# A two-layer hybrid decoder step: layer 0's SSM tables on VectorE, modulation blocks issued earlier, the softmax and gelu stage in another order

## The reference

```python
mod = silu(c) @ w_ada + b_ada;  shift, scale, gate = split(mod, 3)
h = rms_norm(x, norm_g) * (1 + scale) + shift
q, k, v, za, u, zs = split(h @ w_in)              # 512,128,128,512,512,512 columns
ya = windowed attention with sinks(rope(q), rope(k), v)     # prompt, and samples with a cache
# SSM: 32 groups of 16 channels, 64 complex states
abar = exp(a * dt);  bb = coef * b                # coef from a and abar
h_t = abar * h_{t-1} + bb u_t;  y = Re(c h_t) + d * u
y = gelu(y);  y = y * sigmoid(y @ w_glu + b_glu)
x = x + gate * (concat(ya * silu(za), y * silu(zs)) @ w_out)
```

## Time and profile before

| | |
|---|---|
| median of three runs | 457.63 us |
| the profiled execution | 457.97 us |
| its span on the core | 456.2 us |
| TensorE busy (matmuls) | 379.3 us, 83% |
| VectorE busy | 320.4 us, 70% |
| ScalarE busy | 199.9 us, 44% |
| GpSimd busy | 143.1 us, 31% |
| mean granted clock of TensorE | 0.934 of 2.4 GHz |

### The profile page before, as it was taken

How to read it: one execution, slowest core, us unless ns; L and a number is a source line. 1 busy time by engine, 2 the same in 40 slices (tenths; PEclk the granted TensorE clock), 3 DMA queues, 4 the chain that set the end, 5 groups by cost and what they waited for, 6 DMA issues and landing times. The chain is left out here.

```text
span 456.2 us, 8245 instructions
## 1 busy us (share of the span) xinstructions
PE 379.3 (83%) x3114; PEld 320.7 (70%) x3114; DVE 320.4 (70%) x670; ACT 199.9 (44%) x429; POOL 143.1 (31%) x153
## 2 busy tenths in 40 slices
PE   3997289999755993946979967799997999899894
PEld 2444279889652983634869866699996879688893
DVE  1547989488999547298667885536578966986763
ACT  3635084353431226137514345634651348583442
POOL 4400000999930049994069950000000000000320
PEclk9999769999988997987998987999998998999999
DMA  8798878967139537932197407139099628923303
GB/s 270 224 329 294 185 269 238 139 123 229 49 70 279 97 59 220 375 76 63 35 295 255 93 0 214 53 97 175 4 225 205 155 41 235 309 61 86 94 0 116
DMA packets 124869, 72.27 MB, mean 158 GB/s; under 512 B 63129, under 2 KB 111349, under 8 KB 124734
## 3 DMA queue, kind: packets, MB, share of 16 engines
q1 hardware_dynamic: 112462, 65.74, 55.0%
q10 hardware_dynamic: 12368, 6.00, 5.5%
HBM read 64.74 MB, written 6.59 MB: 156 GB/s over the span
## 5 line engine op out<-in xcount | busy, mean ns | idle before, releaser
L655 PE MATMUL bank<-h_hi,w_hi 128*128 128x320 f32 x448 | 146.8, 328 | 22.0 <-DVE w_lo L1598 13.6
L655 PE MATMUL bank<-h_lo,w_hi 128*128 128x320 f32 x448 | 142.0, 317 | 0.0
L655 PE MATMUL bank<-h_hi,w_lo 128*128 128x320 f32 x448 | 141.8, 317 | 0.0
L655 PEld LDWEIGHTS bank<-h_hi,w_hi 128*128 128x128 f32 x448 | 87.6, 196 | 32.0 <-DVE w_lo L1598 16.3
L1598 DVE TENSOR_TENSOR w_lo<-raw,w_hi 128x1024 fp32r<-128x1024 f32 x50 | 67.7, 1354 | 30.3 <-ACT w_hi L1196 30.2
L655 PEld LDWEIGHTS bank<-h_lo,w_hi 128*128 128x128 f32 x448 | 87.7, 196 | 0.2
L655 PEld LDWEIGHTS bank<-h_hi,w_lo 128*128 128x128 f32 x448 | 87.4, 195 | 0.0
L1196 ACT ACTIVATE w_hi<-raw 128x1024 fp32r<-128x1024 f32 x50 | 52.6, 1052 | 37.3 <-PE bank L655 31.3
L2125 POOL TENSOR_TENSOR ga<-xT,fing 128x320 f32<-128x320 f32 x4 | 3.8, 950 | 160.5 <-DVE xT L2002 160.5
L2106 POOL TENSOR_TENSOR pt<-Apow,Csb 128x288 f32<-128x288 f32 x64 | 52.6, 842 | 2.5
L655 PE MATMUL bank<-R,cT 128*32 128x512 f32 x128 | 24.1, 722 | 13.0 <-DMA R<-in_w_ada 12.9
(11 more groups left out here) (266 smaller groups left out, 665.7 us busy)
## 6 DMA issues: line engine op xcount, KB each, us to landing
R<-in_w_ada SPq DMA_DIRECT2D x32, 512.0 KB, 6.6
raw<-in_w_in SPq DMA_DIRECT2D x32, 256.0 KB, 6.0
raw<-in_w_ada SPq DMA_DIRECT2D x14, 512.0 KB, 5.5
raw<-in_w_in SPq DMA_DIRECT2D x14, 512.0 KB, 5.7
raw<-in_w_out SPq DMA_DIRECT2D x32, 128.0 KB, 3.1
raw<-in_w_out SPq DMA_DIRECT2D x16, 256.0 KB, 4.1
R<-in_w_in SPq DMA_DIRECT2D x4, 512.0 KB, 6.9
raw<-in_w_glu SPq DMA_DIRECT2D x4, 512.0 KB, 8.3
```

What stands on the lines that cost most here:

```text
L655: return nc.tensor.matmul(out_, lhsT, rhs, start=start, stop=stop, skip_group_check=free)
```

## The change

- **Tables of layer 0.** Gm of layer 0 is computed on VectorE by `carriers(q)`, four calls of five 128x576 operations each, in place of GpSimd. Three calls follow rope 0, 1 and 2, the fourth follows the modulation of layer 1. WB and Gm use three products in place of four for a complex product, with sums prepared beforehand (`Asd`, `Cdif`, `outputs_summed`). Bblk of layer 0 is copied by ScalarE. GpSimd prepares only layer 1, behind `H_ready` and, for WB, behind the last `mix_ready` of layer 0.
- **Start.** `ssm_sines` and `powers` come ahead of the wait for the spread root; `inputs_scaled` and all `turned_inputs` come after the last `h_lo`. The second half of u0 and u1 comes ahead of turning C and the sinks.
- **Modulation and transfers.** The block (0, 4) is loaded behind zs0 in place of zs1, in layer 1 (1, 4) behind za0 in place of za2; `load_quad` comes ahead of `y_turns`; layer 0's skewing all comes behind zs1. K0 of layer 0 is formed ahead of za1.
- **Softmax and gelu.** ScalarE stores the state ahead of the second exponentials. VectorE does the first gelu steps ahead of the first normalization and of silu 5. PT4, PT5 and the turned modulation 5 come behind glu; layer 1's modulation 2 comes one unit earlier.

```diff
-QUAD_LOADS = ({"q1": 0, "za2": 1, "zs1": 2, "zs3": 3, "glu1": 4, "out5": 5}, {"za2": 0, "glu1": 1})
+QUAD_LOADS = ({"q1": 0, "za2": 1, "zs0": 2, "zs3": 3, "glu1": 4, "out5": 5}, {"za0": 0, "glu1": 1})
-SKEW_AT = (["zs0", "zs0", "zs0", "zs0", "zs1", "zs1", "zs1", "zs1"],
+SKEW_AT = (["zs1"] * T,
...
+            def carriers(q):
+                i0, shape = 4 * q, [P, 4, T + 1, GC]
...
+                step.add(tt(im, A(Asd[:, 1]), C(Csb[:, 0, 0]), ALU.mult))
+                step.add(tt(t, A(Apow[:, 0, 1]), C(Csb[:, 0, 1]), ALU.mult))
+                own(tt(t2, A(Apow[:, 0, 0]), C(Cdif), ALU.mult))
+                own(tt(re, im, t, ALU.add))
+                if q < 3:
+                    own(tt(im, im, t2, ALU.add))
...
                 newton(l + 1)
+                if l == 0:
+                    powers()
                 dve.wait_ge(*work.ready(l, "rb"))
...
                 if l == 0:
+                    inputs_scaled()
+                    for m in range(4):
+                        lo_part(0, m + 2)
+                        turned_inputs(m)
...
                     rope(m)
+                    if l == 0:
+                        carriers(m)
                 lo_part(l, 9)
                 if l + 1 < DEPTH:
                     modulation_of(l + 1, 0)
+                if l == 0:
+                    carriers(3)
...
                 modulation_of(l, 4)
-                normalize(0)
-                silu(5, "zs1", gs[:, 1, :])
-                lo_part(l, 17)
-                normalize(1)
                 dve.wait_ge(y_back, (l + 1) * 64)
...
                 gelu_argument(0)
                 gelu_argument(1)
-                silu(6, "zs2", gs[:, 2, :])
-                lo_part(l, 18)
+                normalize(0)
+                silu(5, "zs1", gs[:, 1, :])
+                lo_part(l, 17)
                 gelu_product(0)
                 gelu_product(1)
                 gelu_argument(2)
                 gelu_argument(3)
+                normalize(1)
+                silu(6, "zs2", gs[:, 2, :])
+                lo_part(l, 18)
+                if l + 1 < DEPTH:
+                    modulation_of(l + 1, 2)
                 gelu_product(2)
                 gelu_product(3)
+                silu(7, "zs3", gs[:, 3, :])
+                for m in range(MT):
+                    gelu_lo(m)
```

More of the change, by code:

```diff
@@ L638, in _ @@
                     u_turns(l)
+                if unit in QUAD_LOADS[l]:
+                    load_quad(l, QUAD_LOADS[l][unit])
                 if unit == "zs3":
@@ L1400, in _ @@
                         .then_inc(y_out, 16)
[L1401 to L1406, removed]
                 act.wait_ge(*work.ready(l, "at4"))
@@ L1418, in _ @@
                         .then_inc(state_stored, 16)
-                gelu_square(0)
-                gelu_square(1)
-                gate(6, "zs2")
-                hi_part(l, 18)
-                gelu_tanh(0)
-                gelu_tanh(1)
+                exponentials(1)
+                gate(4, "zs0")
+                hi_part(l, 16)
                 if l + 1 < DEPTH:
@@ L1723, in _ @@
                         else:
-                            powers()
-                            inputs_scaled()
-                            for n in range(2):
-                                turned_inputs(n)
                             modulation_of(0, 2)
@@ L1752, in _ @@
                         .then_inc(ada.emptied(0, "sinks"), 1)
-                    for m in range(4):
-                        lo_part(0, m + 2)
-                        turned_inputs(m + 4)
+                    outputs_summed()
                     dve.wait_ge(rest_in, 16)
@@ L2086, in all_turned @@
-                def all_turned():
-                    for n in range(8):
-                        turned(n)
-                if before is not None:
-                    pool.wait_ge(*work.ready(before, "y3"))
+                X, Y = flat(Csb[:, own_, 0]), flat(Csb[:, own_, 1])
+                Ar, Ai = flat(Apow[:, own_, 0]), flat(Apow[:, own_, 1])
+                Bsum, Bdif = flat(Bsb[:, own_, 0]), flat(Bsb[:, own_, 1])
+                pool.wait_ge(ssm_ready, 1)
+                pool.wait_ge(wb_ready, l * 8)
@@ L2114, in prepare @@
-                if before is not None:
-                    pool.wait_ge(*work.ready(before, "pvs"))
-                    all_turned()
-            prepare(0, None)
-            for before in range(DEPTH - 1):
-                step.restart()
-                prepare(before + 1, before)
+                    t, t2 = (pt[:, q, 0:2 * (T + 1) * GC].rearrange("p (i s c) -> p i s c", i=2, s=T + 1)
+                             for q in range(2))
+                    re, im = (Gm[:, r, i0:i0 + 2] for r in range(2))
@@ L2123, in _ @@
+            for l in range(1, DEPTH):
+                prepare(l)
             for k in range(KT):
```

245 lines of the change are left out of this document (139 added, 106 removed).

## The result

The changed kernel takes 441.84 us (median of 4 runs, 440.94 to 444.44) beside 457.71 us of the kernel before (4 runs, 456.24 to 462.36): ratio 0.9646, 95% interval 0.9566 to 0.9725. It is faster, by 15.9 us. The same kernel was timed again later (six runs): 444.24 us, ratio 0.9766 (0.9718 to 0.9815). So its gain is 11 to 16 us, and single edits are compared best within one set of runs. The repeat was expected at 440 to 443 us and came out above that. Medians here are over all runs; the ratios leave out runs that are over 1.5% above the fastest of their kernel. The profiled execution took 441.92 us, span 440.0.

The account below looks back on a forecast made before the run. No engine bounds the whole: TensorE is busy most of the span and stops at a few places of layer 0. Terms -3.7 + 9.4 - 16.5 + 0.3 - 11.2 + 2.5 = -19.2, from 457.97 us to 439 us, range 430 to 451.

Parts of the forecast that it names:

- step 3: k to `carried`: scan shorter without GpSimd's tables beside it, block (0, 4) in time; -16.5 us, bounds -18 and -8.
- steps 4 and 5: `carried` to y3: late skewing, +0.3 us; y3 to values: earlier work and blocks, -11.2 us, bounds -18 and -3.
- Start: Start to u2: u0 4.3 us later, last modulation earlier, u2 at 63.9 not 67.61; -3.7 us, bounds -6 and 0.
- u2 to k: `carriers` on VectorE, 3.75 us a call, delays k from 105.7 to 111.4; +9.4 us, bounds 0 to +21.
- Out stage: Values' end to layer 0's sum of squares: no term of its own, left at the 40.1 us of before.
- Layer 1: Layer 1: state stored ahead of exponentials, zs3 waits 3.2 us more; +2.5 us, bounds -1 and +6.
- dear tables: Rival: `carriers` cost 6 us a call, all through S4 and the scan, +9; 448 us, chance 0.22.
- That the blocks land late: Rival: blocks load only after the one before is used, so 4.49 and 7.01 us waits stay; 451 us, chance 0.06.
- y was back in time: Answers the rival that VectorE stands at `y_back`, with work queued behind, and the change loses; 463 us, chance 0.05.
- more gain: Rival: zs3 doesn't wait (-4), no clock loss at 42 (-1.8), layer 1 free (-2.5); 431 us, chance 0.15.

Follow-up runs that it names:

- experiment 5: Changed kernel with sines and `powers` back behind the normalisation, tables still on VectorE: 442.74 us, beside 444.24 for the changed kernel in the same set.
- experiments 3 and 4: Changed kernel with, first, layer 0's Gm on GpSimd in five-operation form without `carriers`: 438.11 us; second, three `carriers` calls one place earlier: 438.18 us.
- experiment 1: Changed kernel plus 40 GpSimd multiplies that nothing reads, between layer 0's reading tables and the scan's end: 465.38 us, ratio 1.0145.
- experiment 2: Changed kernel with modulation blocks loaded at their old places, skewing split over zs0 and zs1, y's way back ahead of block (1, 2): 455.16 us.
- experiment 7: Changed kernel with block (1, 2)'s load issued behind y's transfers on SyncE, not ahead: 442.69 us, ratio 0.9669.
- first execution: First profiled execution of the changed kernel, without further edit: 441.92 us.
- second execution: Another profiled execution of the same changed kernel, from its later repeat, whose median was 444.24 us.
- experiment 8: Changed kernel with GpSimd starting layer 1's WB when pvs is there, as before, not behind the mix: 443.92 us, ratio 0.9700.
- experiment 6: Changed kernel with the old softmax and gelu order in both layers: 442.04 us; with the new order in layer 0 only: 439.12 us.

## Why the prediction was right

Forecast 439.0 us with 430 to 451; measured 441.84, and 444.24 later. The kernel is faster, as the chance of 0.92 had it, and both medians lie in the range, the second just past the forecast's own range of 434 to 444. The mechanism of the large term (step 3) was right; two smaller terms were too hopeful (steps 4 and 5), and a stage that was put at no change gave 3 us back, which was luck.

1. *Start.* -3.7 forecast, -3.4 measured; u0 started at 40.8 and not 42.2. Right in sum, wrong in what brings it. I had `powers` ahead of `normed` as half of the gain. With `powers` late and the scaled inputs and tables still moved, u2 starts earlier still (61.56 to 63.12), so it was those that had held up the last modulation; `powers` early costs 1 to 3 us (experiment 5).
2. *u2 to k.* +9.4 forecast; 111.0 less 64.2 is 46.8, before 38.0: +8.8. The price of a call was as forecast. Of the three stops, two came with the releasers named: 2.01 us for `HY` (h0; forecast 2.7) and 2.73 us for the modulation (forecast 4.4); the third, for rope2 (1.2), is 0.3 us at most. It is the price of the change, and experiments 3 and 4 take 3 to 9 us of it away.
3. *k to `carried`.* -16.5 forecast, measured 31.2 us after 48.5: -17.3. Block (0, 4) was issued at 124.6 and no wait stood behind za2 or zs0. By experiment 1 GpSimd's idleness gives the scan; by experiment 2 that alone would leave TensorE waiting 7.51 us for the block. The Trainium skill (SBUF — State Buffer, SBUF: two separate sides) has a VectorE instruction with two SBUF inputs and a GpSimd instruction that reads SBUF block each other; the trace agrees, with 213 against 601 ns for the same instruction (experiment 1).
4. *`carried` to y3.* The step that failed. Forecast +0.3, measured +3.5. It had one term, skewing that lands a microsecond late; no wait for Toep stands there in the trace. Block (1, 2)'s load was weighed only as a risk for y's way back, and put at nothing for TensorE. 2.5 us are the stop, 0.9 a wait for the modulation at 145.06. Without the load the stop goes, but the time stays (experiment 7).
5. *y3 to the values.* Forecast -11.2 us, measured -6.0 in the first execution and -6.8 in the second. In size this is the largest miss, 5.2 and 4.4 us. The wait ahead of zs3 was forecast at 6.3 and is 6.19. Not foreseen: a wait of 1.92 us for turned probabilities, and smaller ones; TensorE idles 9.2 us of the stage, and 10.0 in the second execution, with 1.5 us for gelu's `h_lo` (up to 3.5 us in other profiles). And the clock: with 0.83 over the stage the same work took 51.5 us in the first execution, beside 49.3 before; in the second it took 49.9.
6. *Out stage*, which the forecast left at 40.1: 36.6 and 37.4. These unforeseen 3 us cover more than half of what step 5 lacks. Experiment 8 shows one part of it, the rest is open.
7. *Layer 1.* +2.5 forecast, +1.6 and +2.4 measured; up to +5.1 in variants with the same layer 1 (experiment 6).

Of the rivals, dear tables is out (3.8 us a call, not 6). That the blocks land late is out for the change; experiment 2 brings it back. y was back in time: no wait for it stands in VectorE's way. Of more gain, one condition came true by experiment: without the new order in layer 1 it is 439 us, not 431.

## What to carry to other kernels

Undo each part of a bundle: here one part (loads issued earlier) is worth 8 to 13 of the 11 to 16 us once the rest is in, one shows no gain (the new gelu order in layer 0), and three cost 1.5 to 6 us each by the medians, which the bundle hid: Gm on VectorE, early powers (1.5, not clear of the noise) and the new order in layer 1. Work that is moved into an engine's idle time may still cost, if the stop it makes stands ahead of matmuls that then run slowly, or if it slows the engine beside it (experiment 1). A stop that shows nothing to wait for should be looked for in the DMA view; and before it is mended, look at what would be waited for next.

## What the runs showed of the hardware

- VectorE's instructions of 32 elements took 213 and 222 ns with GpSimd idle, 601 and 648 ns beside a stream of GpSimd multiplies of 1.1 us each; the slowdown of the whole scan was 1.9.
- VectorE's work in the scan took 26.7, 33.6, 38.0 and 51.4 us with GpSimd busy for 0, 13.7, 23.2 and 38.4 us in it.
- TensorE stopped for 2.15 to 2.50 us, at one place of its program, in the eight profiles in which a load was moving over 400 GB/s in the third microsecond before it went on; in the six others, where the load was elsewhere or over, it stopped there for 0.3 us at most.
- The low clock (1.2 GHz) came behind different stops in two executions of one kernel (0.76, 0.90, 1.00 and 0.99, 0.82, 0.92 in the same three stretches). The medians of this kernel in two sets of runs were 441.84 and 444.24 us.
